# The expert passes of a two-block transformer: the next expert's tokens fetched by an indirect row transfer and transposed, and the turned pick matrix built from slot numbers

## The reference, cut to what matters

```python
logits = xt @ w_router                                  # 256 tokens, 8 experts
top_vals, top_idx = lax.top_k(logits, 2)
top_w = jax.nn.softmax(top_vals, axis=-1)
combine = sum(one_hot(top_idx, 8) * top_w[..., None], axis=1)
for e in range(8):
    y = y + combine[:, e:e + 1] * ((silu(xt @ w_gate[e]) * (xt @ w_up[e])) @ w_down[e])
```

## Time and profile before

| | us |
|---|---|
| median of three executions (2162.72 to 2166.65) | 2163.91 |
| the profiled execution's own time | 2160.77 |
| its span, first to last instruction | 2158.9 |
| PE busy (share of the span) | 2109.3 (98%) |
| DVE busy | 1553.7 (72%) |
| ACT busy | 1173.5 (54%) |
| POOL busy | 9.8 (0%) |

### The profile page before, as it was taken

The page is one execution under the profiler, slowest core; times in us unless marked ns, Lnnn a source line. Parts: engine busy times, 40 slices in busy tenths (PEclk is TensorE's granted clock), DMA queues, the critical chain, the costliest instruction groups (busy, mean ns, idle before and its releaser), DMA issues.

```text
span 2158.9 us, 33161 instructions
## 1 busy us (share of the span) xinstructions
PE 2109.3 (98%) x12570; PEld 1843.9 (85%) x12570; DVE 1553.7 (72%) x1823; ACT 1173.5 (54%) x1201; POOL 9.8 (0%) x22
## 2 busy tenths in 40 slices
PE   7999999999899989999999999999999999999997
PEld 6888799999898989989897888888888888888885
DVE  8677356555646454464648989898998889899897
ACT  3301135434447234434726777777777777777774
POOL 0000000000000000000000000000000000000000
PEclk9999999999999999999999999999999999999999
DMA  8343343555552445565345989899898989899893
GB/s 314 128 154 138 116 156 119 180 190 184 211 210 99 156 157 194 178 232 179 115 141 229 373 344 365 356 361 362 344 361 347 361 346 362 347 366 369 347 357 155
DMA packets 76181, 540.01 MB, mean 250 GB/s; under 512 B 9136, under 2 KB 9280, under 8 KB 11952
## 3 DMA queue, kind: packets, MB, share of 16 engines
q1 hardware_dynamic: 71856, 522.22, 63.1%
q0 software_dynamic: 2080, 10.40, 1.3%
q10 hardware_dynamic: 2144, 5.93, 0.7%
HBM read 537.47 MB, written 1.05 MB: 249 GB/s over the span
## 4 chain that ended last, share of the span: by engine, by line
PE 88%; DVE 8%; ACT 2%; issue 2%; DVEq 1%; DMA 0%; ACTq 0%
PE psum L1316 14%; PE psum L916 12%; PE psum L1293 10%; PE psum L1297 9%; PE psum L1296 9%; PE psum L756 6%; PE psum L929 5%; PE psum L728 5%; PE psum L694 4%; PE psum L681 2%; DVE scan_t L2198 2%; DVE scan_t L2201 1%; DVE big L2204 1%; PE psum L707 1%; PE psum L741 1%
## 5 line engine op out<-in xcount | busy, mean ns | idle before, releaser
L2419 DVE TENSOR_TENSOR w_l<-ring,w_h 128x2048 fp32r<-128x2048 f32 x336 | 768.9, 2291 | 103.9 <-ACT w_h L1497 98.0
L1497 ACT ACTIVATE w_h<-ring 128x2048 fp32r<-128x2048 f32 x336 | 645.4, 1921 | 131.8 <-PE psum L1293 92.5
L1293 PE MATMUL psum<-w_h,xe_h 128*128 128x512 f32 x896 | 359.2, 401 | 0.9 <-DVE w_l L2419 0.9
L1297 PE MATMUL psum<-w_h,xe_l 128*128 128x512 f32 x896 | 349.9, 390 | 0.0
L1296 PE MATMUL psum<-w_l,xe_h 128*128 128x512 f32 x896 | 349.4, 390 | 0.0
L2029 DVE TENSOR_TENSOR wf_l<-ring,wf_h 128x2048 fp32r<-128x2048 f32 x66 | 151.1, 2291 | 135.7 <-ACT wf_h L1488 135.7
L2000 DVE TENSOR_TENSOR wp_l<-ring,wp_h 128x2048 fp32r<-128x2048 f32 x52 | 119.0, 2290 | 116.1 <-ACT wp_h L1511 116.1
L1293 PEld LDWEIGHTS psum<-w_h,xe_h 128*128 128x128 f32 x896 | 168.3, 188 | 37.0 <-DVE w_l L2419 4.2
L1297 PEld LDWEIGHTS psum<-w_h,xe_l 128*128 128x128 f32 x896 | 168.2, 188 | 35.9
L916 PE MATMUL psum<-xf_h,wf_h 128*128 128x256 f32 x688 | 195.8, 285 | 1.6 <-DVE xf_l L2037 1.6
L1296 PEld LDWEIGHTS psum<-w_l,xe_h 128*128 128x128 f32 x896 | 168.7, 188 | 31.8
(11 more groups left out here) (423 smaller groups left out, 3668.6 us busy)
## 6 DMA issues: line engine op xcount, KB each, us to landing
ring<-in_stream SPq DMA_DIRECT2D x497, 1024.0 KB, 5.8
big<-in_bc POOLq DMA_DIRECT2D x11, 512.0 KB, 8.1
big<-in_na_bias POOLq DMA_DIRECT2D x2, 2048.0 KB, 9.0
h<-in_x SPq DMA_DIRECT2D x2, 512.0 KB, 4.3
big<-in_mem ACTq DMA_DIRECT2D x1, 1024.0 KB, 12.3
big<-in_s_c ACTq DMA_DIRECT2D x1, 1024.0 KB, 13.0
r_k<-in_sgu_ln ACTq DMA_DIRECT2D x1, 1024.0 KB, 17.5
out_dram<-ysum ACTq DMA_DIRECT2D x2, 512.0 KB, 2.6
```

What stands on the lines that cost most here:

```text
L1293: first = nc.tensor.matmul(out, xe_h[:, k, :], wh[:, i, :], start=(k == 0), stop=False)
L1297: last = nc.tensor.matmul(out, xe_l[:, k, :], wh[:, i, :], start=False, stop=(k == KD - 1))
L1497: nc.scalar.activation(high, src, ACT.Copy).then_inc(w_high, 1)
L2419: V.tensor_tensor(low, src, high.bitcast(F32), ALU.subtract).then_inc(w_split, 1)
```

## The change

1. The 32 gather products of the next pass at s = 12 are gone (the first pass keeps its own, as `first_gather`). In their place PE waits for `rows_ready` and transposes 8 pieces of 128 x 128 of `tok_rows` (`turn_rows`).
2. `tok_rows` (128 slots x 1024) is filled by GpSimd with an indirect transfer of 128 rows of 4 KB out of `h_rows`, a copy of the tokens in device memory, which GpSimd stores once before the passes. The loop has a fixed count of 10; DVE frees all that are left in the last pass.
3. The row numbers come from `slot_numbers`: two float32 products on PE of `pick` with `tok_no` (token number + 1, in two equal columns), at s = 10 and once more at s = 4 of the first pass. DVE reads the result (`read_slots`) at the chunk down 9 as `slot_f` and as the integer `slot_i`, and frees GpSimd.
4. `pickT` is built by DVE from `slot_f` and a row of token numbers, `tok_row`, at the chunk down 7. The two transposes of `pick` on PE and ACT's `move_pickT` are gone.
5. Once, in the second layer's mixer, DVE computes `tok_no` and `tok_row`.

The diff's core:

```diff
+INDEX_AT = PICK_AT + 2
@@ block.gpsimd, after norm_load(1, 1, 6)
+            pool.wait_ge(xn_ready, 8)
+            pool.dma_start(h_rows.rearrange("(b p) d -> p b d", p=P), h[:, :, :]).then_inc(rows_stored, 16)
+            pool.wait_ge(rows_stored, 16)
+            for p in range(MOE_E + OVER - 1):
+                pool.wait_ge(no_ready, p + 1)
+                if p > 0:
+                    pool.wait_ge(rows_ready, 16 * p)
+                pool.indirect_dma_start(out=tok_rows, out_offset=None, in_=h_rows[:, :],
+                                        in_offset=bass.IndirectOffsetOnAxis(ap=slot_i[:, 0:1], axis=0)
+                                        ).then_inc(rows_ready, 16)
+            pool.wait_ge(rows_ready, 16 * (MOE_E + OVER - 1))
@@ block.tensor
-            def transpose_pick():
+            def slot_numbers():
                 for b in range(TB):
-                    last = nc.tensor.transpose(psum[:, 2 + PICK_AT % 2, b * P:(b + 1) * P], pick[:, b, :].bitcast(F32), ident[:, :])
-                last.then_inc(pickT_full, 1)
+                    last = nc.tensor.matmul(psum[:, 6, 0:2], pick[:, b, :].bitcast(F32), tok_no[:, b, :],
+                                            start=(b == 0), stop=(b == TB - 1))
+                last.then_inc(no_full, 1)
+
+            def turn_rows():
+                for k in range(KD):
+                    last = nc.tensor.transpose(psum[:, 6 + k // 4, (k % 4) * P:(k % 4 + 1) * P],
+                                               tok_rows[:, k * P:(k + 1) * P], ident[:, :])
+                last.then_inc(gathered, 1)
@@ one_expert on PE
-                    if s == GATHER_AT and not last_pass:
+                    if s == 4 and first:
+                        slot_numbers()
+                    if s == INDEX_AT and not last_pass:
                         pe.wait_ge(pick_ready, p + 2)
                         pe.wait_ge(y_added, p * 4 + 4)
-                        gather(1)
+                        slot_numbers()
+                    if s == GATHER_AT and not last_pass:
+                        pe.wait_ge(rows_ready, p * 16 + 16)
+                        turn_rows()
@@
-                        if s == PICK_AT + 1:
-                            pe.wait_ge(pickT_ready, p + 1)
                         transpose_h(p, s - 1)
-                    if s == PICK_AT:
-                        transpose_pick()
@@ one_expert on ACT
-                        if s == PICK_AT - 2:
-                            move_pickT(p + 1)
@@ block.vector, mixer m == 1
+                    link(V.reduce_sum(tok_no[:, 0, 0:1], before, AX_X))
+                    link(V.tensor_scalar(tok_no[:, 0, 0:1], tok_no[:, 0, 0:1], -1.0, float(P), ALU.mult, ALU.add))
+                    link(V.tensor_copy(tok_no[:, 0, 1:2], tok_no[:, 0, 0:1]))
+                    V.tensor_scalar(tok_no[:, 1, :], tok_no[:, 0, :], float(P), None, ALU.add)
+                    for b in range(TB):
+                        V.tensor_scalar(tok_row[:, b * P:(b + 1) * P], iota, float(b * P + 1), None, ALU.add)
@@
+            def read_slots(n):
+                dve.wait_ge(no_full, n)
+                last = V.tensor_copy(slot_f[:, :], psum[:, 6, 0:1])
+                if not (isinstance(n, int) and n == 1):
+                    last = V.tensor_scalar(slot_i[:, :], psum[:, 6, 0:1], -1.0, 0.0, ALU.add, ALU.max)
+                    last.then_inc(no_ready, 1)
@@ one_expert on DVE
-                        if s == PICK_AT - 1 and not last_pass:
-                            dve.wait_ge(gathered, p + 1)
-                            dve.wait_ge(pickT_full, p + 1)
-                            build_pick(p, lambda b: pass_pos[:, b, bass.ds(p + 1, 1)])
+                        if s == PICK_AT - 1:
+                            dve.wait_ge(y_added, p * 4 + 4)
+                            V.tensor_scalar(pickT[:, :, :].rearrange("p b m -> p (b m)"), tok_row, slot_f[:, 0:1], None,
+                                            ALU.is_equal).then_inc(pickT_ready, 1)
+                            if last_pass:
+                                V.memset(msq[:, :], 0.0).then_inc(no_ready, MOE_E + OVER - 1)
+                            else:
+                                build_pick(p, lambda b: pass_pos[:, b, bass.ds(p + 1, 1)])
+                        if s == INDEX_AT - 1 and not last_pass:
+                            read_slots(p + 2)
+                        if first and s == 4:
+                            read_slots(1)
```

More of the change, by code:

```diff
@@ L276, in build @@
         warm = sb("warm", [P, 1])
+        tok_no = sb("tok_no", [P, TB, 2])
+        slot_f = sb("slot_f", [P, 1])
+        slot_i = sb("slot_i", [P, 1], I32)
+        h_rows = nc.dram_tensor("h_rows", (TOK, D), F32, kind="Internal").ap()
         lam_a = sb("lam_a", [P, 2, 2, BLK])
@@ L392, in build @@
         nabias = view(big, 7168, 4096, "p (h b m) -> p h b m", h=8, b=TB)
+        tok_rows = big[:, 8192:9216]
+        tok_row = big[:, 9216:9472]
         bc = view(big, 11264, 4096, "p (n d) -> p n d", d=D)
@@ L482, in build @@
         oe_half_split = sem("oe_half_split")
-        pickT_full = sem("pickT_full")
+        rows_stored = sem("rows_stored")
+        no_full = sem("no_full")
+        no_ready = sem("no_ready")
+        rows_ready = sem("rows_ready")
         pickT_ready = sem("pickT_ready")
@@ L1238, in _, with first_gather @@
             all_banks_free(len(UNITS))
-            def gather(n):
+            def first_gather():
                 for k in range(KD):
@@ L1250, in gather @@
                                                     start=(b == 0 and part is h_h), stop=(b == 1 and part is h_l))
-                            if n == 0 and k == b == 0 and part is h_h:
+                            if k == b == 0 and part is h_h:
                                 last.then_inc(scattered, 2 * TB)
-                    if n == 0 and k == 3:
+                    if k == 3:
                         last.then_inc(gathered_half, 1)
                 last.then_inc(gathered, 1)
-            def transpose_pick():
+            def slot_numbers():
                 for b in range(TB):
-                    last = nc.tensor.transpose(psum[:, 2 + PICK_AT % 2, b * P:(b + 1) * P], pick[:, b, :].bitcast(F32), ident[:, :])
-                last.then_inc(pickT_full, 1)
+                    last = nc.tensor.matmul(psum[:, 6, 0:2], pick[:, b, :].bitcast(F32), tok_no[:, b, :],
[6 more added lines that the diff above has]
+                last.then_inc(gathered, 1)
             def scatter_half(b, c, bank_n):
@@ L1368, in _ @@
             pe.wait_ge(pick_ready, 1)
-            gather(0)
+            first_gather()
             one_expert(0, True)
@@ L1778, in move_xe @@
                                      ACT.Copy).then_inc(xe_high, 1)
-            def move_pickT(n):
-                act.wait_ge(pickT_full, n)
-                nc.scalar.activation(pickT[:, :, :], halves(psum[:, 2 + PICK_AT % 2, 0:TOK]), ACT.Copy).then_inc(pickT_ready, 1)
             def move_oe(n):
```

## The result

The changed kernel took 2219.78 us (2218.95 to 2220.79, four runs) against 2163.31 us in the same comparison: a ratio of 1.0267, interval 1.0255 to 1.0279. That is 56.5 us more, where 22.4 more were forecast, and above the range. The sign and the mechanism were as forecast; the loss was two and a half times as large. The experiments were measured in two further sets of runs, in which the kernel before took 2161.44 us (PE without the wait, the direct load, DVE keeps off, the fetch one step earlier) and 2164.41 us (the others), so a difference in microseconds between two sets holds to about 3 us, and the ratios are the safer comparison.

The account below looks back on a forecast made before the run. PE was taken to bound the passes alone. Per fetch -2.37 us of PE work, +4.5 of wait and +1.0 of clock gave +3.1; seven, with the first pass's 0.44, made +22.4: 2186 us, 8-in-10 range 2157 to 2207.

Parts of the forecast that it names:

- PE's own work: PE, per fetch: gather and pick transposes gone, row transposes and slot-number products added, -2.37 us in sum.
- The cover: Between GpSimd's release by DVE and PE's arrival at its wait after step 12's products: 3.1 us.
- The landing: GpSimd's fetch lands 7.3 us after issue, 7.6 after the release, so PE waits 4.5 us.
- The clock: PE behind each wait: granted clock falls to 0.50, costing +1.0 us per fetch, ends 0 and 2.
- The episode taken as a model: Half clock ahead of the passes, from about 1142.3 to 1145.5, read as 3.2 us, 1 us within the wait.
- The rest at 0: DVE's compare and reads, mixer instructions, GpSimd's 1 MB store, fetch traffic and spare fetches: all costed at 0.
- Rival 1: GpSimd's issue held up by DVE's two-input low part, starting 2.3 us later: 6.8 us wait, 2202 us; chance 0.20.
- The Trainium skill's fit for a GpSimd transfer: Fetch time as 2.0 us plus bytes over 436 GB/s: 3.2 us for 512 KB, wait about 0.4 us, 2151 us.

Follow-up runs that it names:

- PE without the wait: Changed kernel, but PE transposes tokens already in SBUF and does not wait for the still-running fetch: 2147.17 us, ratio 0.9930 to the kernel before.
- the direct load: Changed kernel with GpSimd's indirect fetch replaced by a plain load of the first 128 stored rows, same 512 KB: 2201.46 us, ratio 1.0182 to the kernel before.
- DVE keeps off: Changed kernel with two unused one-input row sums on DVE after its two reads, before the next low part: 2205.62 us, ratio 1.0202 to the kernel before.
- the fetch one step earlier: Changed kernel with the whole fetch moved one step earlier, PE still turning the rows at s = 12: 2150.30 us, ratio 0.9941 to the kernel before.
- the gather kept beside the fetch: Changed kernel with the gather products back in place of the row transposes, the fetch running unwaited: 2166.42 us, ratio 1.0011 to the kernel before.

## Why the prediction was wrong in size

- **PE's own work, -2.37 us per fetch.** Right: 123.80 to 121.43 without the wait, though two parts were off by 0.19 us each and cancel.
- **The cover, 3.1 us.** Nearly right: 3.4.
- **The landing, 7.3 us from the issue. This step failed.** It was 10.6. The price was taken from a direct load beside a stream; the text named a longer issue as the reason why the end lay above 8.3, and then gave it no price. A direct load at this very place lands in 8.3 us (six of seven fetches), so the traffic was undersized by 1.0. The indirect form adds 2.3: 0.2 for its longer own issue, and 2.1 for GpSimd held up by DVE, as the landings without the hold (8.5 us on average in those six) show. The wait was 7.6 us and not 4.5: 3.1 x 7 = 22 us.
- **The clock, 1.0 us per fetch. Undersized, too.** Take the distance from one set of transposes to the next, less 121.43 and less the wait: it was 2.9 to 3.0 us where half clock lasted 5.7 us behind the wait, and 1.9 where it lasted 3.5, some 16.5 us in all seven and not 7. The stated upper end was 2. The episode taken as a model lasted 3.4 us (1142.45 to 1145.87; the prediction read 3.2); the one shown lasted from about 1397.1 to 1407.3, of which 5.7 us lay behind the wait. The length of the wait does not explain the price: behind waits of 5.2 to 5.6 us (DVE keeps off) half clock lasted 5.3 to 5.9 us, behind waits of 7.5 to 7.8 us 3.5 or 5.7. Why it alternates stays open.
- **The rest at 0.** Right within 0.2 us per pass, by the gather kept beside the fetch (0.40 more, of which 0.21 was forecast as PE's work).
- **Rival 1, GpSimd held up by DVE.** Its mechanism was real (2.1 us of the stated 2.3), but it stood as an alternative to the forecast with a chance of 0.20 and a time of 2202 us. In truth it came on top of an undersized landing and an undersized clock; a range that adds the bad ends of the three terms would have reached 0.3 + 8.3 + 2.3 - 3.1 = 7.8 us of wait and 2 us of clock, 7.4 per fetch, 52.4 in all: 2216 us on the median, near what came, though the clock's true ends were higher than 2.
- **The Trainium skill's fit for a GpSimd transfer** (DMA: Bandwidth & Descriptors, Anatomy of one DMA — SWDGE path), 3.2 us by its formula, was far off in these passes: 8.3 us direct and 10.6 indirect. The formula has no term for a stream that keeps the DMA engines 0.90 busy.

In sum: -16.6 + 0.4 + 53.0 + 16.5 = 53.3 of the 56.5 us measured. The rest lies ahead of the passes and is not the change: the first gate product starts at 1155.2 before and at 1159.7 in the changed kernel, but in the other traces, whose code up to there is nearly the same, it starts anywhere from 1155.4 to 1162.3.

## What to carry to other kernels

Where one engine bounds and never waits, a fetch that replaces some of its work is worth that work, as long as it is issued early enough: here the same code loses 2.7% with 3.4 us of cover and gains 0.6% with one step more. Read the cover from the order of time, between the release and the consumer's arrival, hold against it the fetch's landing under the stream's load, and add the ends of costs that can come together: here the hold of GpSimd, the traffic and the clock all fell on the same wait. Price the fall of the clock from its own episodes, for it did not grow with the wait.

## What the runs showed of the hardware that was not expected

- GpSimd's indirect issue of 128 rows takes 0.95 us, and up to 3.04 us where DVE has started an instruction with two SBUF inputs before it; in all ten issues of the changed kernel it ended 0.81 to 0.87 us after that instruction. Where the issue started 0.14 us ahead of DVE's instruction, both took their usual time. A direct issue took 0.53 us beside the same instruction. Giving DVE 2.3 us of useless one-input work made the kernel 14.2 us faster.
- After the end of the issue the first packet came 3 us later beside a backlog of the ring, and the fetch then had a third of the engines. The last spare fetch of the changed kernel, with the ring at its end, landed in 5.7 us against 10.6.
- Useless products in a wait of 7.6 us brought 17.8 us (2.5 per wait), by keeping the clock at 1.00. Without them half clock lasted 3.5 or 5.7 us behind waits of the same length.
